# Two mixing blocks: attention levels between the streamed projections, decayed factors in one array per level, masks as predicated copies

## The reference

```python
u, q, k, v, g_out, a_low = jnp.split(h @ w_in, IN_SPLITS, axis=-1)
log_alpha = log_sigmoid(a_low @ w_alpha_up + b_alpha) / 16      # per token and key channel
# gated linear attention, 4 heads, keys of 64, values of 128; b = running sum of log_alpha
scores[i, j] = sum_d q[i, d] * k[j, d] * exp(b[i, d] - b[j, d])   # j <= i
o = rms_norm(scores @ v, head_gain) * silu(g_out)
# S5: diagonal complex recurrence of 2048 states over 512 channels
states[t] = lam_bar * states[t-1] + b_bar @ u[t];  y = real(c_mat @ states) + d * u
y = gelu(y);  y_s5 = y * sigmoid(y @ w_glu + b_glu)
mix = concat(y_s5, o) @ w_out
```

## Time and profile before

| | |
|---|---|
| median of 3 runs | 2970.05 us (2966.34 to 2970.11) |
| the profiled execution | 2976.95 us, its span 2975.2 us |
| busy: PE, DVE, ACT, POOL | 89%, 75%, 49%, 32% of the span |
| granted PE clock, mean over the span | 0.925 of full |
| HBM read | 667.82 MB, 225 GB/s over the span |
| sub-block 6 (mixer) | about 1121 to 1350 us |
| sub-block 8 (mixer) | about 1648 to 1879 us |
| sub-block 9 (experts) | the last third |

### The profile page before, as it was taken

The page is one execution under the profiler, slowest core; times in us unless marked ns, Lnnn a source line. Parts: engine busy times, 40 slices in busy tenths (PEclk is TensorE's granted clock), DMA queues, the critical chain, the costliest instruction groups (busy, mean ns, idle before and its releaser), DMA issues. The chain is left out here.

```text
span 2975.2 us, 47277 instructions
## 1 busy us (share of the span) xinstructions
PE 2657.4 (89%) x17674; PEld 2414.6 (81%) x17674; DVE 2241.1 (75%) x2501; ACT 1465.4 (49%) x1886; POOL 941.0 (32%) x568
## 2 busy tenths in 40 slices
PE   7998689999998897568997756799999999999997
PEld 7998489999988887348997633699999999999986
DVE  6676566766767755877777677589888888988888
ACT  4343443433444334114333311477777777777765
POOL 6970059788408301324999142000000000000000
PEclk9999599999999998689998858899999999999999
DMA  8764067677444453025773301499999999999986
GB/s 292 250 209 149 22 226 248 217 248 253 168 186 156 162 176 131 25 68 208 255 241 114 131 22 54 164 344 344 336 346 344 341 345 331 342 343 341 344 311 228
DMA packets 129207, 670.56 MB, mean 225 GB/s; under 512 B 14672, under 2 KB 14992, under 8 KB 80064
## 3 DMA queue, kind: packets, MB, share of 16 engines
q1 hardware_dynamic: 111024, 604.72, 55.6%
q0 software_dynamic: 18064, 64.21, 6.3%
HBM read 667.82 MB, written 1.05 MB: 225 GB/s over the span
## 5 line engine op out<-in xcount | busy, mean ns | idle before, releaser
L1595 PE MATMUL work<-xT_hi,wh_gu 128*128 128x256 f32 x2120 | 611.2, 288 | 57.1 <-DVE xT_lo L871 25.2
L1596 PE MATMUL work<-xT_lo,wh_gu 128*128 128x256 f32 x2120 | 608.7, 287 | 0.0
L1597 PE MATMUL work<-xT_hi,wl_gu 128*128 128x256 f32 x2120 | 608.0, 287 | 0.0
L1595 PE MATMUL work<-wh_gu,mixT_hi 128*128 128x256 f32 x1792 | 513.0, 286 | 4.7 <-DVE mixT_lo L1317 3.2
L1596 PE MATMUL work<-wl_gu,mixT_hi 128*128 128x256 f32 x1792 | 505.7, 282 | 0.0
L1597 PE MATMUL work<-wh_gu,mixT_lo 128*128 128x256 f32 x1792 | 505.4, 282 | 0.0
L754 DVE TENSOR_TENSOR wl_gu<-raw_gu,wh_gu 128x2048 fp32r<-128x2048 f32 x158 | 390.2, 2469 | 124.3 <-ACT wh_gu L378 123.8
L1595 PEld LDWEIGHTS work<-xT_hi,wh_gu 128*128 128x128 f32 x2120 | 415.7, 196 | 68.5 <-issue 39.7
L1596 PEld LDWEIGHTS work<-xT_lo,wh_gu 128*128 128x128 f32 x2120 | 416.4, 196 | 4.8
L1597 PEld LDWEIGHTS work<-xT_hi,wl_gu 128*128 128x128 f32 x2120 | 415.5, 196 | 0.0
L1595 PE MATMUL acc<-wh_d,h_hi 128*128 128x512 f32 x912 | 379.6, 416 | 4.5 <-DVE wl_d L1329 2.7
(11 more groups left out here) (438 smaller groups left out, 4873.8 us busy)
## 6 DMA issues: line engine op xcount, KB each, us to landing
raw_gu<-in_w_gu SPq DMA_DIRECT2D x271, 1024.0 KB, 4.9
raw_d<-in_w_d SPq DMA_DIRECT2D x269, 512.0 KB, 5.4
scratch<-in_w_gu SPq DMA_DIRECT2D x112, 1024.0 KB, 7.2
scratch<-in_w_d SPq DMA_DIRECT2D x112, 512.0 KB, 7.8
scratch<-in_w_mod POOLq DMA_DIRECT2D x96, 512.0 KB, 3.7
scratch<-in_s_b POOLq DMA_DIRECT2D x16, 256.0 KB, 2.9
rows<-in_norm_post POOLq DMA_DIRECT2D x6, 512.0 KB, 4.4
rows<-in_ln_g POOLq DMA_DIRECT2D x4, 512.0 KB, 4.0
```

The lines of the kernel that those rows point to most:

```text
L1595: pe.matmul(out_, w[0], m[0], start=start, stop=False)
L1596: pe.matmul(out_, w[0], m[1], start=False, stop=False)
L1597: return pe.matmul(out_, w[1], m[0], start=False, stop=stop)
```

## The change

All of it is in `mix2` and its parts; unit contents and the loads of weights stay the same.

- PE: `stream` replaces `unit` for U to U+5. The gate logits follow directly behind unit U+1, and the diagonal term and the levels 0 to 7 stand one each behind the blocks v1, go0, go1, go2, go3, u0, u1, u2 and u3. u goes to `acc` banks. S5's first input stands ahead of scores times v, the second one behind it.
- ACT now copies q, k, gate input, v and u out of PSUM (`keep`, `keep_u`), takes the Silu of g_out straight from PSUM, and has the `hi` of the coming units between the Exps.
- DVE: `decayed` multiplies in place the lower half of each pair with k and the upper half with q, so a level has one array `DF` and not three, and POOL's sixteen multiplications go. Each level's scores are written over `SC` by two predicated copies with the mask. `lo` of units U+4, U+5 and U+6 stands behind levels 0, 3 and 6, the C matrices are prepared ahead of the attention, and the scaling by root and gate is one pass in S5's round 0 (`gated_heads`); the low parts come in round 1 (`mixed_heads`).
- POOL multiplies g_out by the head gain and loads C early; its first two loads of B wait for the last `decayed`. `hi` of U+7 moves ahead of the squares.

```diff
@@ PE, mix2 @@
-                unit(U, [T, T, T])
...
-                unit(U + 5, [T, None, T])
+                def level(j):
+                    if j < 0:
+                        pair_scores(QG, KG, 0).then_inc(g["scores"], 1)
+                        return
+                    pe.wait_ge(g["decayed"], 8 * n + j + 1)
+                    x = DF[j % 3]
+                    if j:
+                        pe.wait_ge(g["masked"], 9 * n + j)
+                        pair_scores(x, x, (j + 1) % 2).then_inc(g["scores"], 1)
+                        return
...
+                stream(U, t_[0:3])
+                stream(U + 1, [t_[3], t_[4], v[0]])
+                alpha()
+                stream(U + 2, v[1:4], (-1, None, None))
+                stream(U + 3, go[0:3], (0, 1, 2))
+                stream(U + 4, [go[3], u_[0], u_[1]], (3, 4, 5))
+                stream(U + 5, [u_[2], None, u_[3]], (6, None, 7))
...
                 bu(0)
+                heads()
                 bu(1)
-                pe.wait_ge(mix_l, MSTART[b] + 2)
+                heads_transposed()
@@ DVE, mix2 @@
+                lo(U + 1)
+                if b > SECOND:
+                    residual(b)
+                lo(U + 2)
...
+                link(STT(CS[:, 2], CT[0], -1.0, CT[1], ALU.mult, ALU.subtract))   # last of 7 for C
                 dve.wait_ge(g["z"], n + 1)
...
                 STT(LT, BT, -1.0, BT, ALU.mult, ALU.max).then_inc(g["zabs"], 1)
+                lo(U + 3)
...
+                def decayed(j):
+                    df = halves(j, DF[j % 3])
+                    dve.wait_ge(g["exp"], 8 * n + j + 1)
+                    TT(df[:, :, 0, :], df[:, :, 0, :], halves(j, KG)[:, :, 0, :], ALU.mult)
+                    TT(df[:, :, 1, :], df[:, :, 1, :], halves(j, QG)[:, :, 1, :], ALU.mult).then_inc(g["decayed"], 1)
...
+                            here = masks[:, j - 1:j, :].broadcast_to([P, 4, P]).bitcast(I32)
+                            last = dve.copy_predicated(SC[:, w], here, ps)
...
+                differences(0)
+                differences(1)
+                masked(-1)
+                decayed(0)
+                for j in range(8):
+                    if j + 2 < 8:
+                        differences(j + 2)
+                    if j + 1 < 8:
+                        decayed(j + 1)
+                    masked(j)
+                    if j in (0, 3, 6):
+                        lo(U + 4 + j // 3)
@@ ACT, mix2 @@
+                decay(0)
+                decay(1)
+                act.wait_ge(d_used, U + 3)
+                act.activation(VG, PA[:, 0:2, :], ACT.Copy).then_inc(g["vg_sb"], 1)
+                hi(U + 4)
+                decay(2)
+                decay(3)
+                decay(4)
+                hi(U + 5)
+                decay(5)
+                decay(6)
+                keep_u(0, gu_used, U + 5)
+                decay(7)
+                act.wait_ge(gu_used, U + 5)
+                act.activation(GO, PA[:, 2:4, :], ACT.Silu).then_inc(g["gout"], 1)
+                keep_u(1, d_used, U + 5)
+                hi(U + 6)
@@ POOL @@
+                    pool.wait_ge(g["gout"], n + 1)
+                    pool.wait_ge(headgain_in, 16 * (n + 1))
+                    TT(GO, GO, HG.unsqueeze(1).broadcast_to([P, NT, 512]), ALU.mult).then_inc(g["gained"], 1)
+                    pool.wait_ge(g["decayed"], 8 * (n + 1))
                     for r in range(2):
                         pool.dma_start(SBM[r], A["s5_b"][n, r]).then_inc(s5b_in[r], 16)
```

More of the change, by code:

```diff
@@ L206, in program @@
+        PP = [view(4608 + 512 * i, 512) for i in range(4)]
+        TURNED = [[ROW[:, 512 * i:512 * i + 512] for i in range(4)],
+                  [ROW[:, 2048:2560], HG, first_net[:, 0:512], first_net[:, 512:1024]]]
+        YT = view(6656, 1024).rearrange("p (k s) -> p k s", k=4)
         GL = view(2048, 1024).rearrange("p (k s) -> p k s", k=4)
@@ L592, in mix2 @@
                 act.activation(LT, LT, ACT.Ln, bias=ones).then_inc(g["zexp"], 1)
-                for j in range(8):
-                    act.wait_ge(g["diff"], 2 * (8 * n + j + 1))
-                    act.activation(DF[j % 3], DF[j % 3], ACT.Exp, scale=1.0 / 16.0).then_inc(g["exp"], 1)
+                decay(0)
[15 more added lines that the diff above has]
+                hi(U + 6)
+                keep_u(2, gu_used, U + 6)
+                keep_u(3, d_used, U + 6)
+                hi_gu(U + 7)
                 act.wait_ge(g["o"], n + 1)
@@ L1161, in gla @@
[L1161 to L1170, removed]
@@ new lines, in masked @@
+                    pair = (j + 1) % 2
+                    for w in range(2):
+                        ps = PB[:, 2 * pair + w, :].rearrange("p (h i) -> p h i", h=4)
+                        if j < 0:
+                            last = TT(SC[:, w], ps, ident.unsqueeze(1).broadcast_to([P, 4, P]), ALU.mult)
+                        else:
+                            here = masks[:, j - 1:j, :].broadcast_to([P, 4, P]).bitcast(I32)
+                            last = dve.copy_predicated(SC[:, w], here, ps)
@@ L1194, in skip, with gated_heads @@
                     dve.wait_ge(s["y"], 8 * n + 2 * t + 2)
-                    STT(YT[:, t, :], UT[:, t, :], C("s5_d", 4 * n + t), PB[:, t, 0:S],
+                    STT(YT[:, t, :], UT[:, t, :], C("s5_d", 4 * n + t), s5_output(t)[:, 0:S],
                         ALU.mult, ALU.add).then_inc(s["ysum"], 1)
+                def gated_heads():
+                    dve.wait_ge(g["root"], n + 1)
+                    link(dve.reciprocal(grs, grs))
+                    dve.wait_ge(g["gained"], n + 1)
+                    for t in range(NT):
+                        for h in range(4):
+                            v = slice(h * P, (h + 1) * P)
+                            last = STT(OG[:, t, v], PB[:, t, v], grs[:, 4 * t + h:4 * t + h + 1], GO[:, t, v],
+                                       ALU.mult, ALU.mult)
+                    last.then_inc(g["og"], 1)
+                    dve.wait_ge(g["og"], n + 1)
@@ L1198, in s5, with mixed_heads @@
+                def mixed_heads():
+                    for t in range(NT):
+                        tok = slice(t * P, (t + 1) * P)
+                        mix_lo(ML[:, 4:8, tok], PB[:, t, :].rearrange("p (k s) -> p k s", k=4), MH[:, 4:8, tok])
                 PP3 = [x.rearrange("p (t s) -> p t s", t=2) for x in PP]
@@ L1205, in turn_in @@
                     er, ei = table_pair(r)
[L1206 removed]
+                    vr, vi = (s5_input(r, c).rearrange("p (t s) -> p t s", t=2) for c in range(2))
                     dve.wait_ge(s["bu"], R + 1)
@@ L1867, in mix2 @@
-                for h in range(4):
-                    v0, v1 = (VG[:, t, h * P:(h + 1) * P] for t in range(2))
-                    o = slice(h * P, (h + 1) * P)
-                    odd, r = h % 2, h // 2
-                    pe.matmul(PB[:, 0, o], SC[:, odd, r, :], v0, start=True, stop=True)
-                    pe.matmul(PB[:, 1, o], SC[:, 2, 2 * odd + r, :], v0, start=True, stop=False)
-                    last = pe.matmul(PB[:, 1, o], SC[:, odd, 2 + r, :], v1, start=False, stop=True)
-                last.then_inc(g["o"], 1)
@@ L1875, in mix2, with stream, then @@
-                pe.wait_ge(g["og"], n + 1)
-                for t in range(NT):
-                    for k in range(4):
-                        last = pe.transpose(PB[:, 2 + t, k * P:(k + 1) * P], OG[:, t, k * P:(k + 1) * P], ident)
-                    last.then_inc(g["oT"], 1)
+                def stream(u, parts, behind=(None, None, None)):
+                    def then(i):
+                        if behind[i] is not None:
+                            level(behind[i])
+                    pe.wait_ge(gu_lo, u + 1)
+                    last = parts[0](u, 0)
+                    if parts[1] is None:
+                        last.then_inc(gu_used, 1)
+                    then(0)
+                    if parts[1] is not None:
+                        parts[1](u, 1).then_inc(gu_used, 1)
+                    then(1)
+                    pe.wait_ge(d_lo, u + 1)
+                    parts[2](u, 2).then_inc(d_used, 1)
+                    then(2)
@@ new lines, in mix2, with heads @@
+                t_, u_ = [t_block(i) for i in range(5)], [u_block(i) for i in range(4)]
+                stream(U, t_[0:3])
[5 more added lines that the diff above has]
+                stream(U + 5, [u_[2], None, u_[3]], (6, None, 7))
+                def heads():
+                    pe.wait_ge(g["masked"], 9 * (n + 1))
+                    for h in range(4):
+                        v0, v1 = (VG[:, t, h * P:(h + 1) * P] for t in range(2))
+                        o = slice(h * P, (h + 1) * P)
+                        odd, r = h % 2, h // 2
+                        pe.matmul(PB[:, 0, o], SC[:, odd, r, :], v0, start=True, stop=True)
+                        pe.matmul(PB[:, 1, o], SC[:, 2, 2 * odd + r, :], v0, start=True, stop=False)
```

(8 more changed lines are left out.)

222 lines of the change are left out of this document (105 added, 117 removed).

## The result

The changed kernel takes 2870.01 us (median of 4, 2865.65 to 2870.82) against 2970.08 beside it: ratio 0.9662, 95% interval 0.9645 to 0.9678. Its profiled execution took 2870.82 us (span 2869.0, PE clock 0.944 against 0.925). The forecast was 2869.

The account below looks back on a forecast made before the run. PE bounds the projection; the attention is a ring of waiting engines, its turn all DVE. Two blocks at 50.5 us give 101: profiled 2976.95 becomes 2876, less 6.9 to the median, 2869 us; range 2862 to 2880, with B and hand-overs 2858 to 2894.

Parts of the forecast that it names:

- S1: Stretch from PE's start of the projection to S5's first product on DVE; predicted near 64 us, not 120.
- Rival B: Predicated copies at 2.5 us for two, or level scores at 2.08 us on PE: 2879 to 2886 us; chance 0.12.
- The loads come 2.5 us too late for DVE: Before S5: loads of B wait behind POOL's product, so bu(0) ends last and S5 starts at 1185.0.
- the ring: The attention's levels, where the engines wait for each other; to be put under the projection, with a shorter turn.
- Given back in S5: Head scaling, reciprocal, waiting and low parts, which stood outside S5 before, lengthen it by 4.7 us a block.
- S2: Stretch from S5's first product on DVE to the end of the last skip; S5 predicted 73 us, not 68.
- hand-overs: DVE's waits on another engine, taken at 0.1 us each, ten on the path: net gain 51.6 becomes 50.5 us.
- The turn of 4.79 us: One turn of the attention's ring before the change, claimed all DVE: subtractions 1.37 + 0.41, masks 1.27, sum 1.86.
- C: Rival: turns don't overlap, each level waits for the whole 8.2 us chain: 2960 us; chance 0.04.
- D: Rival: the ring stops the projection, PE waits at each level and loses its clock: 3016 us; chance 0.03.
- E: Rival: the expert weights stream hides the second block's gain, only sub-block 6 counts: 2919 us; chance 0.03.
- The rule on the shared port: GpSimd and two-SBUF-input VectorE operations exclude each other; POOL's product could hold DVE 2.4 us, sum 99 to 101.

Follow-up runs that it names:

- e4: Changed kernel with PE making the scores of levels 1 to 7 twice, the second over the first: 2882.0 us, ratio 0.9700.
- e5: Changed kernel with DVE making the predicated copies of levels 1 to 7 once more, into an array nobody reads: 2874.7 us, ratio 0.9678.
- e3: Changed kernel with S5's first input matrix B loaded some 25 us earlier, into an array free then: 2870.5 us, ratio 0.9641.
- e1: Changed kernel with each level's mask multiplied into a second array and added, not two predicated copies: 2881.4 us, ratio 0.9702.
- a2: The changed kernel unaltered, measured again beside the runs with idle matmuls: 2873.9 us, ratio 0.9654.
- e10: As e9, plus nine idle matmuls ahead of the gated linear unit and ten ahead of the output projection: 2853.8 us, ratio 0.9584.
- e9: Changed kernel plus PE matmuls nobody reads, ten ahead of S5's round 6 outputs and five ahead of round 7's: 2866.3 us, ratio 0.9635.

## Why the prediction was right

- **PE.** A level costs more than it was priced: its scores took 1.16 us against 1.05, and from one block to the next it added 1.3 us (pitch 4.04 us with a wide block of 2.74, 4.16 with a T block of 2.88); the gate logits took 1.1 against 0.7. That is 2.5 us from the end of v0 on, and v0 ended at 1138.5 and not at 1140.1, of which 0.95 us are PE's earlier start: level 7's scores ended at 1181.45 against 1180.5. That PE sets the pace of S1 is what e4 and e5 show. Rival B's halves (2.08 us a level, 2.5 us a pair of copies) did not come: the value between ends far apart was the right one both times, the copy's the nearest row of the same shape.
- **DVE.** Levels from 1150.5 (predicted 1152.2), last mask ended 1183.3 (1182.3), waits for PE between the levels 4.1 us where I had 1.5, and ahead of S5 0.7 us (none in sub-block 8) where I had 1 to 3: ahead of PE by more, to the same end.
- **POOL and the load.** Product 2.39 us (2.4 to 3.4), loads issued 1178.27. "The loads come 2.5 us too late for DVE: this, not the ring, ends last" failed as a size. The load ended 0.5 us behind PE's last scores, since I had given the product 3 us and PE's end was 1 us later; e3 took the load away for 0.6 and 0.1 us. What ends last is `bu(0)`, at 1183.95, 0.65 us behind DVE's last mask. So the step that named what ends last was mis-sized by 2 us, with no effect on the sum.
- **S1.** 64.1 us forecast, 64.0 and 64.2 measured.
- **Given back in S5.** 4.7 us forecast, 2.0 and 3.2 measured. The 0.9 us of waiting did not come (heads' products took 2.7 us at the high clock where 4.5 stood at the low), and whether the last outputs run at the one level or the other moves S2 by 2.4 us.
- **Sum.** Between the two profiled executions 106.1 us went, not 101: 113.0 in S1 (112.6 forecast), less 5.2 in S2 (9.4 forecast, and 2.2 for hand-overs), less 1.7 elsewhere. Between the medians it is 100.1. The execution of before was 6.9 us above its median, that of after 0.8. So S1 was foreseen, but the last 5 us of the hit are luck: the profiled time came out 5 us under the forecast 2876, and the 6.9 us taken off to get from profile to median were 6 too many. The two errors cancel.
- **Readings of the working.** The turn of 4.79 us is "all of it DVE", but not at DVE's own price: 1.6 us of it are the subtraction and the addition beside POOL. Two products of 1.3 to 2.24 us would be 2.6 to 4.5 us and not 2.4 to 3.4 (measured 2.39), and 1182.8 + 2 is 1184.8 and not 1185.0. Only the last enters the sum, with 0.2 us a block.
- **The other rivals.** C and D (turns in lockstep, PE stopped) are out: PE waits at no level. E is out: behind sub-block 8's S5 the program takes 1137.7 us against 1136.5 and begins that stretch 107 us earlier. The rule on the shared port changed nothing in the changed kernel and cost DVE 2.2 us a block as soon as there was no wait for it to fall into (e1).

## What to carry to other kernels

A ring of four engines put under a PE-bound stretch costs that stretch only PE's own part of it (here some 12 us a block); but price the shorter turn and what can be prepared early by themselves first, since here they brought about four fifths of the gain. When PE is short of work just ahead of a PE-bound burst, look at its granted clock there: idle matmuls in a PSUM bank that nobody needs then delayed nothing and brought 12 us in the traces (20 between the medians). After any retiming compare stretches, not only medians: a burst's clock differed between two executions of one kernel, and the kernel before moved by 7 us between groups. Take a duration as a price only where POOL was idle beside it.

## What was unexpected of the hardware

- A predicated copy of 128x512 from PSUM with an int32 mask takes 0.63 us from start to start (a pair 1.25), as the multiplication of that shape did, and was not longer beside POOL.
- S5's last outputs, 16 matmuls, end 2.2 to 2.5 us sooner or later with the clock level that PE finds (0.38 or 0.63 us each, 2.4 or 1.2 GHz), with the same DVE schedule (to 0.03 us between e3 and the changed kernel). The changed kernel met each level once in one execution. Work of PE's own just before raised it in most cases: the granted clock over the last 12 us of S5 was 0.64 and 0.72 in a2's two blocks, 1.00 in both of e10's, but in one block of e9, with the same matmuls ahead, the last outputs began at the low level. The Trainium skill says that the clock follows how busy PE has recently been (page "TensorE: Matmul & The Clock Gate", part 1), and e10 agrees.
- An addition of 1024 elements takes 1.86 us beside POOL and 1.23 us without it (e1, and the last two levels of the kernel before).
